# The down products of a two-layer trunk as seven block products for eight, with rows combined in pairs and two of gate/up's sums made by an accumulating transfer

## The reference

```python
def swiglu_ffn(x, g, w_gu, w_down):
    h = rmsnorm(x, g) @ w_gu
    a, b = jnp.split(h, 2, axis=-1)
    return (jax.nn.silu(a) * b) @ w_down

def run_trunk(...):
    for layer in range(DEPTH):
        if layer < N_A_LAYERS:
            o, s = hgrn2_mixer(x, ...)
            x = x + o
        else:
            ...
            o = fox_attention(q, k_all, v_all, cq, c_all, q_pos, k_pos)
            x = x + o.reshape(...) @ b_wo[j]
        x = x + swiglu_ffn(x, ffn_norm[layer], w_gate_up[layer], w_down[layer])
```

## Time and profile before

| | us |
|---|---|
| median of 3 runs | 1809.26 (1804.97 to 1809.34) |
| the profiled execution | 1808.28 |
| its span | 1806.5 |
| PE busy | 1741.4 (96%) |
| DVE busy | 1151.8 (64%) |
| ACT busy | 885.1 (49%) |
| POOL busy | 348.6 (19%) |

### The profile page before, as it was taken

How to read it: one execution, slowest core, us unless ns; L and a number is a source line. 1 busy time by engine, 2 the same in 40 slices (tenths; PEclk the granted TensorE clock), 3 DMA queues, 4 the chain that set the end, 5 groups by cost and what they waited for, 6 DMA issues and landing times. The chain is left out here.

```text
span 1806.5 us, 41781 instructions
## 1 busy us (share of the span) xinstructions
PE 1741.4 (96%) x16593; PEld 1616.2 (89%) x16593; DVE 1151.8 (64%) x2113; ACT 885.1 (49%) x1579; POOL 348.6 (19%) x261
## 2 busy tenths in 40 slices
PE   8999999999999999999998999999989999999998
PEld 7999998889999999999997677776769999999998
DVE  4766775579828828555653466666656994595481
ACT  5355445465525524455632455555555653354252
POOL 3333332000120130333531011112200004003012
PEclk9999999899999999999999999999999999999999
DMA  5333222323423332342356999999983334234232
GB/s 129 85 108 85 83 84 66 87 79 94 118 71 94 95 94 71 87 147 62 117 172 205 384 374 379 385 385 367 366 287 99 94 94 117 61 97 115 57 100 70
DMA packets 291541, 273.79 MB, mean 152 GB/s; under 512 B 22034, under 2 KB 252531, under 8 KB 290836
## 3 DMA queue, kind: packets, MB, share of 16 engines
q1 hardware_dynamic: 289412, 268.63, 45.8%
q10 hardware_dynamic: 1792, 1.44, 0.3%
q0 software_dynamic: 144, 1.05, 0.2%
HBM read 254.64 MB, written 16.43 MB: 150 GB/s over the span
## 5 line engine op out<-in xcount | busy, mean ns | idle before, releaser
L2117 PE MATMUL ps<-xh,f_l 128*128 128x288 f32 x1232 | 279.2, 298 | 0.2 <-DVE f_l L2373 0.2
L2137 PE MATMUL ps<-f_h,f_l 128*128 128x288 f32 x1748 | 243.0, 296 | 0.2 <-DVE t_small L2482 0.2
L2137 PEld LDWEIGHTS ps<-f_h,f_l 128*128 128x128 f32 x1748 | 236.1, 189 | 0.4 <-DVE t_small L2482 0.4
L2117 PEld LDWEIGHTS ps<-xh,f_l 128*128 128x128 f32 x1232 | 208.6, 189 | 0.6 <-DVE f_l L2373 0.5
L2117 PE MATMUL ps<-xl,f_l 128*128 128x288 f32 x704 | 208.3, 296 | 0.0
L2117 PE MATMUL ps<-f_l 128*128 128x288 f32 x1056 | 156.8, 297 | 7.6 <-ACT t_small L2264 4.2
L2447 DVE TENSOR_TENSOR xT<-xT,ps 128x576 f32<-128x576 f32 x48 | 36.2, 754 | 197.1 <-PE ps L2137 197.1
L1586 DVE COPY at_kt<-ps 128x512 f32<-128x512 f32 x128 | 88.2, 691 | 109.7 <-PE ps L1289 109.2
L2117 PEld LDWEIGHTS ps<-f_l 128*128 128x128 f32 x1056 | 146.2, 189 | 9.0 <-ACT t_small L2264 5.0
L2117 PEld LDWEIGHTS ps<-xl,f_l 128*128 128x128 f32 x704 | 133.6, 190 | 0.0
L653 POOL TENSOR_TENSOR a_wl<-a_wraw,a_wh 128x1024 fp32r<-128x1024 f32 x32 | 78.5, 2456 | 200.6 <-ACT a_wh L548 185.4
(11 more groups left out here) (434 smaller groups left out, 4064.4 us busy)
## 6 DMA issues: line engine op xcount, KB each, us to landing
xT<-in_cache_k SPq DMA_DIRECT2D x40, 512.0 KB, 6.1
xT<-in_cache_v SPq DMA_DIRECT2D x40, 512.0 KB, 6.6
a_wraw<-in_a_w_in SPq DMA_DIRECT2D x32, 512.0 KB, 4.2
f_h_plain<-in_cache_k SPq DMA_DIRECT2D x30, 512.0 KB, 6.4
xl_plain<-in_cache_v SPq DMA_DIRECT2D x30, 512.0 KB, 6.5
f_h_plain<-in_cache_v SPq DMA_DIRECT2D x30, 512.0 KB, 7.0
xl_plain<-in_cache_k SPq DMA_DIRECT2D x29, 512.0 KB, 6.3
a_wraw<-in_w_gate_up SPq DMA_DIRECT2D x44, 256.0 KB, 4.1
```

Source lines behind the costliest of these rows:

```text
L2117: mm = pe.matmul(place(m, pos), wt[:, at], combination(2 * q, part, b), start=pos in (0, 1, 3) and t == 0 and i == 0, stop=t == len(pairs) ...
L2137: mm = pe.matmul(ps[:, first + a, 0:HALF], wt[:, at], hidden(i, part)[:, a * HALF:(a + 1) * HALF], start=opens and t == 0 and y == 0, stop ...
```

## The change

The down product takes the same form as gate and up. Its four quadrants are now two output tiles by two halves of the columns, and it sums over pairs of hidden tiles. The two hidden tiles of a pair must be combined first (three more blocks of 288 columns beside their four halves), as the input tiles are for gate/up. In parts:

- Chunks are 6, 6, 6 and 4 hidden tiles. A d unit has seven block products of 9 matmuls (chunks of 6) or 6 matmuls (the last). The order is g 0 to 6, four d units, g 7 to 12, four, g 13 to 18, four, g 19 to 21, four.
- DVE: `cross` combines hidden tiles after `multiply`, one instruction for an even tile and three in a chain for an odd one; `low_hidden` writes 2x288 elements for an even tile, 3x288 and 2x288 for an odd one. The four sums and the low parts of d units' weights are DVE's too. `residual` is six instructions (five of 288, one of 576 elements) at positions 0, 1, 2, 4, 5 and 6 in place of two of 576.
- ACT: `round_hidden` waits for `cross` and writes the same two sizes.
- POOL has no low parts any more in the feed-forward part. For a g unit from the third on it starts an accumulating transfer, which adds blocks A22 and A11 (512 KB) onto two copies of A21 and so makes S1 and S3; A21 is fetched twice, so `fetch` issues five transfers for these. DVE makes S2 and S4 there, and all four in d units.
- PE waits in a d unit as in a g unit, with `residual` in the place of the snapshot. At the d unit behind the last g unit the products are reordered (`own`).
- Weight slots: 6 for 7. The hidden tile that belongs to the next chunk is rounded one block of d units later (`deferred`).
- Attention: the prompt's units start at steps 9, 16, 24, 32, 40, 48, 56 and 64.

The core of the diff:

```diff
-    FIRST_UNIT, PAIR_STEPS, PARTS_AT, OUT_AT, TAIL_AT = 15, 7, 4, 5, 6
+    PARTS_AT, OUT_AT, TAIL_AT = 4, 5, 6
+    FIRST_UNIT, LAST_UNIT = 9, KSTEPS
+    STARTS = [FIRST_UNIT + j * (LAST_UNIT - FIRST_UNIT) // (KD - 1) for j in range(KD)]
...
-    chunks = [(0, 8), (8, 16), (16, KF)]
+    chunks = [(0, 6), (6, 12), (12, 18), (18, KF)]
...
-    SLOTS, AHEAD, LEAD, HRING = 7, 5, 4, 9
+    SLOTS, AHEAD, LEAD, HPAIRS = 6, 5, 4, 3
...
+    def by_transfer(m):
+        return kind(KD + m) == "g" and m >= 2
...
+    def deferred(n):
+
+        return n > KD and kind(n) == "g" and kind(n - 1) == "d"
+
+    def entering(n):
+
+        if deferred(n):
+            return UNITS[n][1] - 1
+        i = mixed(n)
+        return None if i is None or kind(n) == "d" and chunk_of[i] != UNITS[n][1] else i
...
+                    wanted = [(A22, 1, 1), (S3, 1, 0), (A11, 0, 0), (A12, 0, 1)]
+                    if by_transfer(m):
+                        wanted = [(A22, 1, 1), (A11, 0, 0), (S1, 1, 0), (S3, 1, 0), (A12, 0, 1)]
                     for dst, a, x in wanted:
                         sp.dma_start(operand(m, dst), block(a, x)).then_inc(fetched[m % 2], 16)
...
-                    if pos in (2, 4, 5):
+                    if kind(n) == "g" and pos in (2, 4, 5):
                         pe.wait_ge(e["snapped"], snap[m, {2: 0, 4: 2, 5: 1}[pos]] + 1)
+                    if kind(n) == "d" and pos in (2, 4, 5):
+                        pe.wait_ge(e["taken"], take[m, {2: 0, 4: 2, 5: 1}[pos]] + 1)
                     if pos == 6:
                         pe.wait_ge(e["taken"], take[m, 4] + 1)
...
+                        if kind(n) == "d" and UNITS[n][2] == 0:
+                            pe.wait_ge(e["hlow"], combined(2 * q) + (1 if b < 2 else 2 if b >= 4 else 3))
...
+                            elif own(n) and pos == 2:
+                                product(n, 3, slice(0, 1))
+                                product(n, 2)
+                                product(n, 3, slice(1, None))
...
+                    if by_transfer(m) and which in (S1, S3):
+                        act.wait_ge(summed_up[m % 2], transfers(m))
+                    elif which in FOLDS:
+                        act.wait_ge(e["folded"], fold_at[m, which] + 1)
...
                 def round_hidden(i):
-                    act.wait_ge(e["product"], i + 1)
...
-                    act.activation(halves(hidden(i, 0)), entered(i), ACT.Copy).then_inc(e["hhigh"], 1)
+                    act.wait_ge(e["hcrossed"], crossings(i) + (3 if i % 2 else 1))
...
+                    for g in groups(i):
+                        act.activation(hidden_group(i, 0, g), source(g), ACT.Copy).then_inc(e["hhigh"], 1)
...
+                def add_operands(n):
+
+                    m = n - KD
+                    pool.wait_ge(fetched[m % 2], fetches(m))
+                    pool.dma_start(operand(m, S1, 2), operand(m, A22, 2), accum_op=ALU.add).then_inc(summed_up[m % 2], 16)
...
                 def low_hidden(i):
-                    dve.wait_ge(e["hhigh"], i + 1)
-                    dve.tensor_tensor(halves(hidden(i, 1)), entered(i), halves(hidden(i, 0)).bitcast(F32), ALU.subtract).then_inc(e["hlow"], 1)
+                    for which, g in enumerate(groups(i)):
+                        dve.wait_ge(e["hhigh"], combined(i) + which + 1)
+                        dve.tensor_tensor(hidden_group(i, 1, g), source(g), hidden_group(i, 0, g).bitcast(F32), ALU.subtract).then_inc(e["hlow"], 1)
...
-                def residual(n, tile):
+                def residual(n, pos):
...
-                        for pos in range(steps(n)):
-                            if pos >= steps(n) - 4:
-                                fold(n + 1, FOLDS[pos - steps(n) + 4])
+                        for pos in range(SPAN):
+                            if pos >= 3:
+                                fold(n + 1, FOLDS[pos - 3])
                             if pos == 0 and mixed(n) is not None:
                                 multiply(mixed(n), n - 1 - KD)
+                                cross(mixed(n), e["product"], e["hcrossed"])
                             if kind(n) == "d":
...
+                                if pos in (0, 1, 2, 4, 5):
+                                    residual(n, pos)
...
-                            if pos == 1 and mixed(n) is not None:
-                                low_hidden(mixed(n))
-                            if heads and n >= TAIL - ROWS and pos == 3:
+                            if pos == 1 and entering(n) is not None:
+                                low_hidden(entering(n))
+                            if kind(n) == "d" and pos == 6:
+                                residual(n, pos)
+                            if heads and n >= TAIL - ROWS and pos == 6:
                                 low(2 * UNITS[n][2])
                                 if UNITS[n][2] > 0:
                                     accumulate(KD + 2 * UNITS[n][2])
```

More of the change, by code:

```diff
@@ L1091, in out_step, with unit_at @@
         return mixed_last[c] + 1
+    def unit_at(n):
+        j = sum(start <= n for start in STARTS) - 1
+        return j, n - STARTS[max(j, 0)]
     def unit_pair(n):
-        j, i = divmod(n - FIRST_UNIT, PAIR_STEPS)
-        return 4 * j + i if 0 <= j < KD and i < 4 else None
+        j, i = unit_at(n)
+        return 4 * j + i if j >= 0 and i < 4 else None
     ring, ordinal = {}, {"act": {}, "dve": {}}
@@ L1873, in trunk @@
         if kind(n) == "d":
-            for tile in sorted(range(2), key=lambda x: closing(n, x)):
-                take[m, closing(n, tile)] = len(take)
+            for pos in (0, 1, 2, 4, 5, 6):
+                take[m, pos] = len(take)
             continue
@@ L2118, in product @@
                                            stop=t == len(pairs) - 1 and i == 2, skip_group_check=True)
[L2119 removed]
+                    if some.stop is None:
                         mm.then_inc(e["multiplied"], 1)
[L2122 to L2139 removed]
@@ L2199, in round_part @@
                     m, pos = step_at[s]
-                    which = block_at(KD + m, pos)
+                    which = PRODUCTS[pos][0]
                     if s >= SLOTS:
@@ L2314, in _ @@
                                 silu(UNITS[n][1])
[L2315 removed]
+                            if heads and n > TAIL - ROWS and pos == 1:
+                                finished(n - 1, 1)
+                            if heads and n >= TAIL - ROWS and pos == 6:
                                 finished(n, 0)
[L2317 to L2318 removed]
+                        if heads and n == TAIL - 1:
+                            finished(n, 1)
                         if heads and n == TAIL - 1:
@@ L2347, in _ @@
                     if n in fast:
-                        if kind(n) == "d":
-                            for pos in range(4):
-                                low_block(n, pos)
+                        if by_transfer(n - KD):
+                            add_operands(n)
                         continue
@@ L2367, in low_part @@
                 def low_part(s):
[L2369 removed]
+                    if s >= STEPS:
                         return
```

225 lines of the change are left out of this document (93 added, 132 removed).

## The result

The changed kernel takes 1876.37 us (median of 4 runs, 1875.26 to 1880.17; the kernel before beside it 1809.15), a ratio of 1.0383 with a 95% interval of 1.0367 to 1.0399. The forecast was 1832 with a range of 1797 to 1866: the sign was right, the size was not; +67 us came for +23. The profiled execution took 1876.57 us, its span is 1874.4.

A forecast was written before the change was run, and what follows sets the result against it. TensorE, busy for 96% of the span, was taken as the bound. Terms -35.2 + 25 + 9 + 8 + 18 - 3 = +22 on 1808.3 gave 1830, stated as 1832 for the median; range 1797 to 1866.

The forecast's parts named there:

- the accumulating transfer: Last d unit of a chunk: TensorE waits for the transfer's chain, 1.4 us in 6 places, +8 us; g units cost nothing.
- L - 3.1: TensorE's wait in a chunk's last d unit, with L the accumulating transfer's time, taken as 4.5 us.
- rival 2: Slower still: the accumulating transfer takes 6.5 us, so last d units and g units wait longer; 1866 us, chance 0.12.
- Odd hidden tiles: 20 g units: chained combinations delay ACT's snapshot, so TensorE waits 1.25 us at block product 4; +25 us.
- From g to d: First d units, 6 places: DVE's late residual makes TensorE wait 1.5 us at block product 2; +9 us.
- Last chunks: Last four d units of each layer: DVE is behind TensorE, 12.8 us lost in layer 1, 5.3 in layer 2; +18.
- Attention: The prompt's units spread over 55 steps for 49 ease the transfer-bound stretch; -3 us, between -9 and 0.
- Rival 1: Faster: engines run blocks ahead and only totals count, so only layer 1's last chunk loses, 13 us; 1784 us, chance 0.20.
- Rival 3: Only part of the waits, as snapshots come earlier than placed: without the 25 us, 1807 us, no change; chance 0.13.

The follow-up runs named there:

- the kernel of 1807.36 us: On the changed kernel: rounding behind the snapshots, DVE's own sums in two g units behind d units, first residual earlier, attention's old starts, transfer in two pieces; 1807.36 us, 1.0002.
- the kernel of 1814.97 us: The kernel of 1807.36 us with scale_gate, multiply and cross behind the fourth residual in the first d unit of the first three chunks; 1814.97 us, 1.0041.
- that of 1855.97: Changed kernel with the rounding behind the snapshots and only an eighth of each of the d units' low parts written by DVE; one run, 1855.97 us.

## Why the prediction was wrong

- **The step that failed** is the accumulating transfer: "L - 3.1", with L = 4.5, 1.4 us in six places, 8 us. It measured 3.6 to 4.7 in these places, 24 us, and 39 with the four g units and the half clock behind it. The mechanism and its place were right; both lengths in it were short. The fetch landed 3.5 us into the unit, and POOL could issue at 3.8, not 3.0 (five blocks took 7.1 us for 6.8, and were asked for 3.6 us ahead of the unit); the transfer took 5.85 us from POOL's issue to DVE's start (1564.43 to 1570.31, less the 0.04 of issue). 3.8 + 5.85 + 0.6 + 0.5 - 7.2 = 3.55, and 3.62 was measured. For a transfer that is alone, 4.5 was right (4.5 to 4.6 in most of the 40), though partly by luck: it was read off plain transfers of 3.6 and 4.3, while a plain one from POOL takes 2.9 and the adding makes it 1.6 times as long, which no row of before could tell. In these six places it landed after 5.8 to 6.3, and what the sum left out goes on beside it there: the next unit's fetch, which SP starts 0.4 to 0.9 us later (likely the cause, as said above, and not shown). By rival 2's length, 6.5, the last d units would have waited 3.4; that rival's price was nearly right there and wrong for the g units, of which only four waited. In these four the sum had the wrong start and not the wrong length: POOL issued 4.0 to 4.7 us into g 3 and g 9, for 2.7 (3.1 to 3.4 in the units of the same kind that did not wait).
- **What was not in the sum** is the clock: 37 us more at 1.2 GHz in the feed-forward parts. All the new stretches lie behind waits of TensorE of 1.9 us or more in a d unit, none behind those of 1.67. The wait of 3.62 in the chain above cost 5.3 with what followed: its d unit took 12.4 us for 8.3, and the g unit behind, 2.6 us of it at half clock, 12.3 for 11.2. The prediction had no term for it.
- **Odd hidden tiles**: the wait was right in place, size and number (1.25 forecast, 1.35 to 1.45 measured). "DVE, which has 1.9 us more to do in an odd unit, is covered by this wait" was right as well, and more than I saw: the wait is what gave DVE its time. Taken away, the time came back at the next place that needs DVE.
- **From g to d** 1.67 for 1.5. **Last chunks** 22 for 18 (14.5 and 7.4 more than before, for 12.8 and 5.3): the first unit takes 12 us for the 10.1 I gave it, its waits 3.9 for 4.5, and 2.6 is the half clock. No run was made that mends the last chunks.
- **Attention**: the sign was wrong. That DMA works at 99% in both stretches said nothing on the order; with earlier units TensorE is idle for 12.5 us ahead of ACT's copies (`at_kt`, above), for 8.5 with the starts of before. Why ACT is later for them was not looked into.
- **Rival 1** (only totals count) failed as a forecast of the changed kernel, but holds for a part of what remains once the places are mended: the kernel of 1807.36 us has 35 us fewer matmuls and lost them again, 13 in six first d units, where DVE is at 99%, and some 22 in the last chunks. The last chunks are not of its kind: in the changed kernel DVE is busy in layer 2's for 28.2 of 32.7 us, and 7 us were lost there all the same.
- **Rival 3** (snapshots come earlier than placed) did not come: the snapshots were awaited in all 20 units.

## What to carry to other kernels

When an engine is busy for nine tenths of a stretch, a wait that its work causes elsewhere may be the only slack it has: count the work of each engine over the whole stretch before a wait is mended, and expect the time to come back at the next place. A transfer put in for an engine's work is a chain (issue, fetch, landing, second transfer, landing); it is measured from the request to the first use at the shortest unit of the schedule, not in the middle, and with the transfers that start beside it there. And a wait of TensorE can cost more than its length, since the clock may be granted at half behind it: 3.6 us cost 5.3 here.

## What the runs showed of the hardware

- An accumulating transfer of 512 KB within SBUF landed 4.5 to 6.4 us after its issue (median 4.6 of 40), a plain one from the same queue after 2.8 to 4.7 (median 2.9). Two accumulating ones of 256 KB, issued one behind the other, landed after 3.4 and 4.8 (medians).
- In the six places where SP asked for five blocks of 256 KB within 1 us of that transfer's issue, it landed after 5.8 to 6.3 us.
- A DVE instruction with both inputs in SBUF took 1.08 us for 0.45 beside a POOL instruction that reads SBUF; one with an input in PSUM kept its 0.455 at most.
- Four waits of 1.97 us in six (the kernel of 1814.97 us), and three of 2.1 to 2.2 in six (that of 1855.97), were followed by a stretch at half clock; waits of 0.8 and 1.0 us in one unit (that of 1807.36) were not, nor any of 1.67. What decides among like waits was not settled.
